# Attention projections of a hybrid decoder step: seven half-size block products for each pair of tiles in place of eight

## The reference, cut to what matters

```python
def attn_project(u, w_in, pos):
    n, l, _ = u.shape
    parts = split_sizes(u @ w_in, ATTN_SPLITS)
    qs = [rope(p.reshape(n, l, ATTN_Q_HEADS, HEAD_DIM), pos) for p in parts[0:3]]
    ks = [rope(p.reshape(n, l, ATTN_KV_HEADS, HEAD_DIM), pos) for p in parts[3:6]]
    vs = [p.reshape(n, l, ATTN_KV_HEADS, HEAD_DIM) for p in parts[6:9]]
    return qs, ks, vs, parts[9]
```

## Time and profile before

| | before |
|---|---|
| runs, us | 1383.43, 1383.54, 1381.88 (median 1383.43) |
| profiled execution, us | 1385.0 from the first to the last instruction; the page gives no other time for it |
| TensorE busy | 1311.0 us, 95% of the span, 11346 matmuls |
| VectorE, ScalarE, GpSimd busy | 789.7, 628.7, 477.1 us |
| bytes moved | 182.63 MB, mean 132 GB/s |

### The profile page before, as it was taken

One profiled execution on the slowest core, in us unless ns is written; L12 is line 12 of the kernel. 1 busy time (PEld: TensorE's weight loads), 2 busy tenths in 40 slices (PEclk: granted clock), 3 DMA queues, 4 the chain that ended last, 5 costly groups with the idle time before them and its releaser, 6 DMA issues. The chain is left out here.

```text
span 1385.0 us, 30373 instructions
## 1 busy us (share of the span) xinstructions
PE 1311.0 (95%) x11346; PEld 1257.9 (91%) x11346; DVE 789.7 (57%) x1524; ACT 628.7 (45%) x1409; POOL 477.1 (34%) x400
## 2 busy tenths in 40 slices
PE   5999999999899999999999997799998999999996
PEld 5999999999899999999999997698997988979995
DVE  4444446453455533654446045577979879697444
ACT  4333333333334333333435244367577666774422
POOL 1545423554224552344633212003335343262011
PEclk9999999999999999999999999699999999999998
DMA  6574442753335633448433252453463635644251
GB/s 189 151 214 109 102 109 86 208 143 97 101 85 166 187 98 91 107 127 267 110 100 87 81 172 70 118 141 109 133 183 112 183 113 163 196 136 117 77 172 65
DMA packets 313415, 182.63 MB, mean 132 GB/s; under 512 B 75232, under 2 KB 302256, under 8 KB 312880
## 3 DMA queue, kind: packets, MB, share of 16 engines
q1 hardware_dynamic: 313264, 180.64, 45.6%
HBM read 155.01 MB, written 46.41 MB: 145 GB/s over the span
## 5 line engine op out<-in xcount | busy, mean ns | idle before, releaser
L1429 POOL TENSOR_TENSOR wlo<-w,whi 128x1024 fp32r<-128x1024 f32 x95 | 228.4, 2405 | 430.0 <-ACT whi L1069 430.0
L906 PE MATMUL at_proj<-uhi,whi 128*128 128x272 f32 x1536 | 335.7, 300 | 5.6 <-POOL wlo L1429 3.1
L906 PE MATMUL at_proj<-uhi,wlo 128*128 128x272 f32 x1536 | 319.7, 290 | 0.0
L906 PE MATMUL at_proj<-ulo,whi 128*128 128x272 f32 x1536 | 319.0, 289 | 0.0
L1069 ACT ACTIVATE whi<-w 128x1024 fp32r<-128x1024 f32 x95 | 100.6, 1059 | 338.0 <-PE at_proj L906 299.9
L906 PEld LDWEIGHTS at_proj<-uhi,whi 128*128 128x128 f32 x1536 | 241.2, 191 | 9.2 <-issue 5.3
L906 PEld LDWEIGHTS at_proj<-ulo,whi 128*128 128x128 f32 x1536 | 243.6, 190 | 0.0
L906 PEld LDWEIGHTS at_proj<-uhi,wlo 128*128 128x128 f32 x1536 | 242.0, 191 | 0.0
L1907 PE MATMUL sd_proj<-uhi,whi 128*128 128x272 f32 x768 | 168.7, 301 | 4.8 <-DVEq L2320 2.2
L1907 PE MATMUL sd_proj<-uhi,wlo 128*128 128x272 f32 x768 | 159.9, 290 | 0.0
L1907 PE MATMUL sd_proj<-ulo,whi 128*128 128x272 f32 x768 | 159.8, 290 | 0.0
(11 more groups left out here) (312 smaller groups left out, 2278.8 us busy)
## 6 DMA issues: line engine op xcount, KB each, us to landing
w<-in_attn_w_in_dram SPq DMA_DIRECT2D x88, 512.0 KB, 4.3
w<-in_ssd_w_in_dram SPq DMA_DIRECT2D x40, 512.0 KB, 4.3
w<-in_attn_w_out_dram SPq DMA_DIRECT2D x16, 512.0 KB, 4.1
sd_h<-in_state_ssm_dram SPq DMA_DIRECT2D x16, 512.0 KB, 6.4
sd_bc<-acs_p SPq DMA_DIRECT2D x16, 512.0 KB, 5.3
out_s_ssm_dram<-sd_h SPq DMA_DIRECT2D x16, 512.0 KB, 3.5
w<-in_ssd_w_out_dram SPq DMA_DIRECT2D x16, 512.0 KB, 3.9
at_k_cache<-in_cache_kv_w_dram SPq DMA_DIRECT2D x384, 16.0 KB, 2.7
```

The lines of the kernel that those rows point to most:

```text
L906: last = pe.matmul(proj[:, r, h, 0:HALF], a[:, r, kk * P:(kk + 1) * P], b[:, kk, h * HALF:(h + 1) * HALF], start=(kk == 0 and a is whi and ...
L1429: pool.tensor_tensor(wlo[:, r], w[:, r], whi[:, r].bitcast(F32), ALU.subtract).then_inc(wlo_ready, 1)
```

## The change

The 88 tiles are taken as 44 pairs. A pair is a 2 x 2 matrix of weight blocks (two halves of the features, two tiles), the tokens are a 2 x 2 matrix (two halves of the features, two halves of the tokens), and the four output blocks are formed from seven block products P1 to P7 (Winograd's form of Strassen's scheme) in place of eight. The sums of token blocks are formed once, in the phase `n0`, and kept as high and low parts (`more`, and the memory of `uhi` and `ulo`); that phase runs the sample rows first and loads four weight tiles, not two. Four sums of weight blocks per pair are formed by VectorE (`combine_w`), one in a new buffer `at_s` and three in place. ACT and GpSimd write high and low parts of 512 columns per product, four products ahead (`LEAD`). Some output blocks are accumulated in PSUM on top of an earlier product, after ACT has copied that to `at_out` (`keep`), and VectorE adds the others (`add`). The rotation now reads `at_out` in SBUF, in three instructions (L1477, L1478, L1480). One list of events with places in units of a product (`attn_events`) sets the order on every engine, and the hardware loop is gone. The keys' cache lies in the memory of `part`, and `q` holds two heads, not four. The output projection keeps its 48 matmuls per tile, with splits of 512 columns.

The core of the diff (places of the attention items in the list are left out):

```diff
+LEAD = 4
...
+def attn_products():
+    order = [("P1", 0), ("P2", 0), ("P1", 1), ("P2", 1), ("P6", 0), ("P5", 0), ("P7", 0), ("P4", 0), ("P3", 0)]
+    for n in range(1, PAIRS - 1):
+        order += [("P6", n), ("P1", n + 1), ("P7", n), ("P5", n), ("P2", n + 1), ("P4", n), ("P3", n)]
+    return order + [(what, PAIRS - 1) for what in ("P6", "P5", "P7", "P4", "P3")]
+PRODUCTS = attn_products()
...
+    for s in range(NPROD):
+        events.append((s + 0.02, ("E", s), None))
+    for b in range(LEAD, NBLOCK):
+        events.append((block_end(b - LEAD) + 0.04, ("H", b), None))
+    for n in range(PAIRS):
+        g, p = divmod(n, NP)
+        first = 7 * n + 8
+        events += [(max(7 * n - 3.5, -0.5 + 4 * n), ("SUM", n, 0), g), (max(7 * n - 2.9, -0.4 + 4 * n), ("SUM", n, 1), g),
+                   (7 * n + 1.7 if n else 3.3, ("SUM", n, 2), g)]
...
+            events.append((first - 0.5, ("R", 2 * p + 1), g))
+        if attn_kind(2 * p)[0] in "QK":
+            events.append((first + 0.1, ("R", 2 * p), g))
+    events += [(7 * (PAIRS - 2) + 2.5, ("LO", 0), None), (7 * (PAIRS - 2) + 5.6, ("LO", 1), None)]
...
-                if q == 0:
-                    pe.wait_ge(wlo_ready, TILES * g + t + 1)
-                    pe.wait_ge(proj_free[r], TILES // PAIR * g + t // PAIR)
-                for kk in range(KD // 4 * q, KD // 4 * (q + 1)):
-                    if isinstance(g, int) and g == NG and t == 0:
-                        pe.wait_ge(part_lo, kk + 1)
-                    for a, b in ((whi, uhi), (whi, ulo), (wlo, uhi)):
-                        for h in range(2):
-                            last = pe.matmul(proj[:, r, h, 0:HALF], a[:, r, kk * P:(kk + 1) * P],
-                                             b[:, kk, h * HALF:(h + 1) * HALF],
-                                             start=(kk == 0 and a is whi and b is uhi),
-                                             stop=(kk == KD - 1 and a is wlo))
-                    if kk < KD - 1 and last_use(None if isinstance(g, int) and g == NG else g, t):
-                        last.then_inc(used, 1)
+            def product(s):
+                what, n = PRODUCTS[s]
+                hi, lo = operand[what]
+                to = proj[:, proj_bank(what, n), 0:HALF]
+                if s >= LEAD:
...
+                else:
+                    pe.wait_ge(c22_ready, n + 1)
+                a_hi, a_lo = part_block(whi, s), part_block(wlo, s)
+                for kk in range(NQ):
+                    at = slice(kk * P, (kk + 1) * P)
+                    for a, b in ((a_hi, hi), (a_hi, lo), (a_lo, hi)):
+                        last = pe.matmul(to, a[:, at], b[:, kk, :],
...
-            def w_high(g, t):
-                act.wait_ge(w_in[t % PAIR], TILES // PAIR * 16 * g + 16 * (t // PAIR))
-                act.activation(whi[:, t % PAIR], w[:, t % PAIR], ACT.Copy).then_inc(whi_ready, 1)
+            def w_high(b):
+                act.wait_ge(slot_done, block_end(b - LEAD) + 1)
+                if b >= NPROD:
+                    o = (b - NPROD) // 2
+                    act.wait_ge(w_loaded[0][o % PAIR], 16 * (PAIRS // 2 + o // PAIR))
+                else:
+                    what, n = PRODUCTS[b]
+                    if what in ("P1", "P2"):
+                        act.wait_ge(w_loaded[n % 2][0], 16 * (n // 2))
+                    elif what == "P4":
+                        act.wait_ge(w_loaded[n % 2][1], 16 * (n // 2))
+                    else:
+                        act.wait_ge(sums_ready, 4 * n + {"P5": 1, "P7": 2, "P6": 3, "P3": 4}[what])
...
+            def combine_w(n, step):
+                a11, a12 = raw(n, 0)[:, 0:BLOCK], raw(n, 0)[:, BLOCK:2 * BLOCK]
+                a21, a22 = raw(n, 1)[:, 0:BLOCK], raw(n, 1)[:, BLOCK:2 * BLOCK]
+                if step == 0:
+                    dve.wait_ge(w_loaded[n % 2][0], 16 * (n // 2))
+                    dve.wait_ge(w_loaded[n % 2][1], 16 * (n // 2))
+                    if n:
+                        dve.wait_ge(wlo_ready, AT["P5", n - 1] + 1)
+                    dve.tensor_tensor(s1[:, :], a21, a22, ALU.add).then_inc(sums_ready, 1)
+                    dve.wait_ge(sums_ready, 4 * n + 1)
+                    dve.tensor_tensor(a21, a11, a21, ALU.subtract).then_inc(sums_ready, 1)
+                elif step == 1:
+                    if AT["P1", n] >= LEAD:
+                        dve.wait_ge(wlo_ready, AT["P1", n] + 1)
+                    dve.wait_ge(sums_ready, 4 * n + 2)
+                    dve.tensor_tensor(a11, s1[:, :], a11, ALU.subtract).then_inc(sums_ready, 1)
+                else:
+                    dve.wait_ge(wlo_ready, AT["P7", n] + 1)
+                    dve.wait_ge(sums_ready, 4 * n + 3)
+                    dve.tensor_tensor(a21, a12, a11, ALU.subtract).then_inc(sums_ready, 1)
...
+            def add(s):
+                what, n = PRODUCTS[s]
+                g, p = divmod(n, NP)
+                half = {"P2": 0, "P3": 1, "P7": 1, "P5": 1}.get(what)
+                if what == "P2":
+                    i, kept, ready, src = 0, p1_kept, c11_ready, proj[:, 3, 0:HALF]
+                elif what == "P3":
+                    i, kept, ready, src = 0, u2_kept, c12_ready, proj[:, 2, 0:HALF]
+                elif s == max(AT["P5", n], AT["P7", n]):
+                    i, kept, ready, src = 1, u3_kept, c22_ready, proj[:, 2, 0:HALF]
+                else:
+                    return
+                dve.wait_ge(slot_done, s + 1)
+                dve.wait_ge(kept, n + 1)
+                x = out[:, n % 2, i, half * HALF:(half + 1) * HALF]
+                kind = attn_kind(2 * p + i)
+                if kind[0] in "KQ":
+                    dve.tensor_tensor(x, x, src, ALU.add).then_inc(ready, 1)
+                elif kind[0] == "V":
+                    d = WINDOWS[kind[1]][1]
+                    dve.wait_ge(kv_rows_ready, 3 * (NW * g + kind[1]))
...
-                dve.tensor_tensor(two(straight[:, :]), halves(x), two(cos[:, :]), ALU.mult).then_inc(turned_ready, 1)
-                dve.tensor_tensor(two(crossed[0:64, :]), x[64:P, :, 0:HALF], two(sin[64:P, :]), ALU.mult) \
-                    .then_inc(turned_ready, 1)
-                dve.tensor_tensor(two(crossed[64:P, :]), x[0:64, :, 0:HALF], two(sin[0:64, :]), ALU.mult) \
-                    .then_inc(turned_ready, 1)
-                dve.wait_ge(turned_ready, 3 * len(ROPED) * g + 3 * n + 3)
-                dve.sem_inc(proj_free[r], 1)
+                    dve.wait_ge(c11_ready, n + 1)
+                if at >= 2:
+                    dve.wait_ge(qk_ready, 2 * (at - 1))
+                over = crossed[:, at % 2, :]
+                dve.tensor_tensor(over[0:64, :], x[64:P, :], sin[64:P, :], ALU.mult).then_inc(turned_ready, 1)
+                dve.tensor_tensor(over[64:P, :], x[0:64, :], sin[0:64, :], ALU.mult).then_inc(turned_ready, 1)
+                dve.wait_ge(turned_ready, 3 * at + 2)
+                dve.tensor_tensor(x, x, cos[:, :], ALU.mult).then_inc(turned_ready, 1)
...
-            def w_low(g, t):
-                r = t % PAIR
-                pool.wait_ge(whi_ready, TILES * g + t + 1)
-                pool.tensor_tensor(wlo[:, r], w[:, r], whi[:, r].bitcast(F32), ALU.subtract).then_inc(wlo_ready, 1)
+            def w_low(b):
+                pool.wait_ge(whi_ready, b + 1)
+                pool.tensor_tensor(part_block(wlo, b), w_block(b), part_block(whi, b).bitcast(F32), ALU.subtract) \
+                    .then_inc(wlo_ready, 1)
```

1145 lines of the change are left out of this document (663 added, 482 removed), and 40 rows, old and new, of tables (ATTN_AHEAD, ATTN_BEHIND, ATTN_ITEMS).

## The result

The changed kernel takes 1542.26 us (median of 4 runs, 1540.02 to 1543.1), the kernel before 1383.21 beside it: a ratio of 1.1149, 95% interval 1.1128 to 1.117. The direction was forecast, the size was not: +159 us against +74, and outside the range.

The account below looks back on a forecast made before the run. TensorE bounds the kernel before; VectorE and GpSimd, excluding each other at SBUF, would bound it after. Terms: 4 x 20.9 - 3 x 3.8 - 4 x 1.5 + 8 - 5 + 5 = +74, giving 1457 us, range 1390 to 1525.

Parts of the forecast that it names:

- the middle stretch: 15 tiles (7.5 pairs) of a head group: from 103.1 to 124 us, VectorE and GpSimd excluding each other, +20.9 per group.
- The loop's gap: TensorE nearly idle for 4 us at the loop's end, then at half clock: about 5 us come back over two rounds.
- the last five pairs: End of a head group, with gates and merge: about +9.5 us (gates -1.5), +4.5 in group 1, merge at nothing.
- here TensorE still decides: -3.8, three times: Five tiles with the previous group's last attention items: exclusive work 49 us, TensorE 54.0, so 3.8 us less, three times.
- the start: Phase `n0` and the first group's opening tiles: +5 us (nothing to 10) and +8 us.
- the opening: First group's first five tiles, with no tail items to cover them: 40.5 us against 30.1 of matmuls and 2.4 of items, +8.
- the sign: What the profile after would show: TensorE waiting for `wlo` many times, over 60 us in total, above all in Q pairs.
- the queues starve each other: Rival: VectorE late makes everything late, then GpSimd idles; middle stretch 135 to 145 us, total 1500 to 1545; chance 0.19.
- The clock: Rival: new waits lower TensorE's granted clock; half its matmuls at half clock need 138 us, total near 1515; chance 0.06.

Follow-up runs that it names:

- e1: Changed kernel with the second operand of VectorE's weight sums and rotations left out, same number, order and waits of instructions: 1423.8 us.
- e16: Kernel before the change plus two unused VectorE sums per tile (176 in all, both inputs in SBUF): 1407.1 us.
- e5: Changed kernel, same computation, with VectorE's wait for the constants moved from the head of its program to its first rotation: 1533.0 us.
- e9: Changed kernel, same computation, with the score items 1.5 products later in the order of events (last window 1.0 and 0.3): 1534.3 us.
- e4: Changed kernel, same computation, with three of a pair's seven low parts (P1, P5, P4) formed by VectorE instead of GpSimd: 1533.2 us.
- e8: Changed kernel, same computation, with ScalarE copying tile halves crosswise and VectorE multiplying by the sine in one instruction, not two: 1528.7 us.
- e12: Changed kernel with e4, e5, e8 and e9 together, and ScalarE's copy of P1 2.6 products later: 1520.6 us.
- e13: e12 with the first three weight sums of a pair 1.2 products earlier in VectorE's order: 1525.6 us.
- e6: Changed kernel with the second operand left out of a pair's four weight sums only, rotations as in the changed kernel: 1477.0 us.

## Why the prediction was wrong

**Right.** TensorE stopped being the bound. VectorE's instructions with two inputs in SBUF and GpSimd's exclude each other (e1 shows that this is the cause of three quarters of the loss). Sums and rotations have means over 1 us, all but the fourth sum; the median low part is 1.30 for 1.25; VectorE's busy time passed 1000; no transfer is waited for in the steady groups; the distance of starts of matmuls on one bank is still 0.126 us (nine in 1.14). Of the middle stretch the sum was right in size: for three pairs 14.3 + 2 x 17.5 = 49.3, with 5% 51.8; measured 52.2 to 52.8 in the four groups. Counted by products, the 7.5 pairs take 129.5 to 130.5 us (103 before), with the merge's stop at their end; 124 was forecast. The loop's gap is gone, and it gave back about what was forecast: the last five pairs are 18.6 and 17.0 us longer in groups 0 and 2, where there was none before, and 13.6 in group 1, where there was. The Trainium skill (SBUF — State Buffer, section Who interferes with whom) states both halves, that two SBUF inputs contend with a GpSimd instruction that reads SBUF and that tensor_reduce never does; e1's 0.72 against 1.20 agrees.

**Wrong: "here TensorE still decides: -3.8, three times".** The stretch with the tail items became 3.3 to 4.1 us longer, not 3.8 shorter. I compared an exclusive sum of 49 with TensorE's 54 and did not add up VectorE's own queue there, as I had done for the middle: 60.5 us busy of 71.6 in the changed kernel. e16 points at the step: 176 sums, nothing else, cost 4.7 us in that stretch and nothing in the middle. e1 gives the other side: with the exclusion gone the stretch is 5.6 us shorter than before (62.4 for 67.9), and TensorE does decide. The miss is 7 to 8 us a group, three times.

**Wrong: the last five pairs of a group.** The forecast's terms make about +9.5 (11.0 for the three pairs with rotation, -1.5 for the gates), and +4.5 in group 1 with the loop's 5 taken off; measured +18.6, +13.6 and +17.0 in groups 0 to 2. I had put the merge at nothing, and three weight sums stand ahead of it in VectorE's queue: TensorE's wait for `at_parted` is 19.3 us over the span, before 1.6. With 8 us at half clock behind each stop, an estimate is 4.7 + 4 = 8.7 us a group, which is the size of the miss.

**Wrong: the start.** "Nothing to 10, I take +5" for `n0` and +8 for the opening. The first K rotation is 32.9 us later. The first product starts at 38.25 and not at 24.08: the token sums and their splits in `n0`, the last of which GpSimd ends at 37.3, cost 14.2 us where I had +5. Behind it there is a wait for constants ahead of VectorE's first work, harmless when its first work was a rotation and not a weight sum; e5 makes the mark 5.2 us earlier and the kernel 9.2 us faster. I had costed no wait there. Part of the rest may be no loss: a K tile is now finished with its pair, so the mark itself comes later.

Together: start and group 0 were forecast at +32 (20.9 - 1.5 + 8 + 5) and came to +73.4; groups 1 and 2 at 13.1 each (20.9 - 3.8 - 1.5 - 2.5) and came to 29.1 and 33.0; the last at 15.6, came to 20.5; with -2.8 for the rest that is 41 + 36 + 5 - 3 = 79, what is missing between 74 and 153.2. By stretches, start and the first three pairs of group 0 miss by about 31, the three stretches with tail items by 22, the last five pairs of groups 0 to 2 by 26. Of the 31 no run shows more than the terms above.

**Wrong in kind: the sign.** "TensorE waits for `wlo` over 60 us": 6.9. The waits stood at the scores. Where they stand is a matter of the written order only: e9 moved them to `wlo` (56.5) for 8 us of gain.

**The rival that came true** is the one with 0.19, "the queues starve each other", 1500 to 1545, in size; in mechanism it was right that low parts, high parts, scores and rotations all come late at once, with one more link (ScalarE's copy of P1) than it had. But it had the middle stretch at 135 to 145 us, which came to 130, so that the total lies in its span is in part luck: the other stretches made up for it. The clock took its part. I had written that the new waits are short, 0.5 us per product; they came in stops of up to 5.2 us, and behind many of them the granted clock was 0.50. The mean clocks make 169 us at half clock, before 61 (twice 0.055 of 1538.2 and twice 0.022 of 1385.0). An estimate from that is that the clock costs at most (169 - 61)/2 = 54 us. No run separates it from the gaps ahead of it.

**What stays open.** Why kernels that move work (e4, e8, e12, e13) gain so little. I summed, up to 1000 us, what VectorE's single instructions took above the fastest twentieth of their kind (same line, tiles and shape): 220 us in the changed kernel, 36 before, 74 in e1, 159 in e6, and still 192, 175, 176 and 176 in e4, e8, e12 and e13. So moving work left most of the waiting. But the sum of the waiting does not give the time either. e8, with 45 us less of it and 90 us less busy time for VectorE, gained 14, while e6, with 61 less, gained 65; and e16 has 137 of it and is only 24 us slower than before. The longer chain over ScalarE may be why; no run shows it.
